# First stream: two of the three conditioning parts multiplied and added on VectorE, with one sum over partitions per 512 columns on TensorE

## The reference, cut to what matters

```python
c_act = jax.nn.silu(c)                       # c: 1 x 2048
mod = c_act @ w_ada[l] + b_ada[l]            # w_ada: 2048 x 12288
sh1, sc1, g1, sh2, sc2, g2 = jnp.split(mod[:, None, :], 6, axis=-1)
...
h = rms_norm(x, g_mix[l])                    # first block
proj = h @ w_in[l]                           # 2048 x 7536: "first stream"
q, k, v, q_idx, k_idx, w_idx = split_cols(p_dsa, DSA_SPLITS)
y_dsa = dsa_mixer(q, k, v, q_idx, k_idx, w_idx, q_gain[l], k_gain[l])
```

## Time and profile before

| | before |
|---|---|
| runs, median (lowest to highest) | 3314.17 us (3312.25 to 3314.31) |
| profiled execution | 3311.56 us |
| its span | 3309.3 us |
| mean granted clock of TensorE | 0.971 |
| first stream ends (last matmul of L302 there starts) | 445.82 us |
| TensorE busy | 3100.6 us, 94% |
| VectorE busy | 2067.7 us, 62% |
| ScalarE busy | 1508.7 us, 46% |

### The profile page before, as it was taken

How to read it: one execution, slowest core, us unless ns; L and a number is a source line. 1 busy time by engine, 2 the same in 40 slices (tenths; PEclk the granted TensorE clock), 3 DMA queues, 4 the chain that set the end, 5 groups by cost and what they waited for, 6 DMA issues and landing times. The chain is left out here.

```text
span 3309.3 us, 43832 instructions
## 1 busy us (share of the span) xinstructions
PE 3100.6 (94%) x17864; PEld 2459.1 (74%) x17864; DVE 2067.7 (62%) x2331; ACT 1508.7 (46%) x1819; POOL 20.1 (1%) x10
## 2 busy tenths in 40 slices
PE   8999957979899999999999998999998999999997
PEld 7888844947677676666688876787776788888886
DVE  4557536354677868685548857765575655555555
ACT  4335422223465656564444455455444444444443
POOL 0000001100000000000000000000000000000000
PEclk9999978989899999999999999999999999999999
DMA  7989876076787879696276653475665655555552
GB/s 270 331 274 329 274 263 249 4 296 233 259 315 267 313 256 341 229 320 212 93 248 209 208 194 126 163 241 172 240 230 191 209 185 190 186 182 190 185 183 76
DMA packets 358321, 739.09 MB, mean 223 GB/s; under 512 B 19977, under 2 KB 118422, under 8 KB 344583
## 3 DMA queue, kind: packets, MB, share of 16 engines
q1 hardware_dynamic: 342916, 711.64, 62.5%
q10 hardware_dynamic: 15236, 25.06, 2.1%
HBM read 710.00 MB, written 26.65 MB: 223 GB/s over the span
## 5 line engine op out<-in xcount | busy, mean ns | idle before, releaser
L286 DVE TENSOR_TENSOR moe_w_lo<-ring,moe_w_hi 128x1024 fp32r<-128x1024 f32 x384 | 464.0, 1222 | 174.5 <-ACT moe_w_hi L276 165.4
L286 DVE TENSOR_TENSOR mx_w_lo<-ring,mx_w_hi 128x1024 fp32r<-128x1024 f32 (+1 forms) x288 | 347.5, 1210 | 307.9 <-ACT mx_w_hi L276 303.7
L276 ACT CAST moe_w_hi<-ring 128x1024 fp32r<-128x1024 f32 x384 | 402.3, 1049 | 285.0 <-PE psum L302 281.3
L276 ACT CAST mx_w_hi<-ring 128x1024 fp32r<-128x1024 f32 (+1 forms) x288 | 297.5, 1037 | 448.0 <-PE psum L302 432.0
L286 DVE TENSOR_TENSOR mlp_w_lo<-ring,mlp_w_hi 128x1024 fp32r<-128x1024 f32 x256 | 313.5, 1225 | 293.1 <-ACT mlp_w_hi L276 292.0
L276 ACT CAST mlp_w_hi<-ring 128x1024 fp32r<-128x1024 f32 x256 | 268.4, 1049 | 418.2 <-PE psum L302 418.2
L302 PE MATMUL psum<-mx_w_hi,mx_a_hi 128*128 128x496 f32 (+1 forms) x1024 | 405.6, 396 | 6.4 <-DVE mx_w_lo L286 4.6
L302 PE MATMUL psum<-mx_w_lo,mx_a_hi 128*128 128x496 f32 (+1 forms) x1024 | 397.6, 388 | 0.0
L302 PE MATMUL psum<-mx_w_hi,mx_a_lo 128*128 128x496 f32 (+1 forms) x1024 | 397.6, 388 | 0.0
L286 DVE TENSOR_TENSOR in_w_lo<-ring,in_w_hi 128x628 fp32r<-128x628 f32 x192 | 155.3, 813 | 185.8 <-ACT in_w_hi L276 184.6
L302 PE MATMUL psum<-in_w_hi,in_a_hi 128*128 128x314 f32 x768 | 244.1, 318 | 1.4 <-DVE in_w_lo L286 1.2
(11 more groups left out here) (596 smaller groups left out, 5594.6 us busy)
## 6 DMA issues: line engine op xcount, KB each, us to landing
ring<-in_w_ada SPq DMA_DIRECT2D x72, 1024.0 KB, 7.6
ring<-in_w_e_gate SPq DMA_DIRECT2D x64, 1024.0 KB, 5.4
ring<-in_w_e_up SPq DMA_DIRECT2D x64, 1024.0 KB, 6.3
ring<-in_w_e_down SPq DMA_DIRECT2D x64, 1024.0 KB, 5.2
ring<-in_w_up SPq DMA_DIRECT2D x64, 1024.0 KB, 5.2
ring<-in_w_down SPq DMA_DIRECT2D x64, 1024.0 KB, 5.1
ring<-in_w_in SPq DMA_DIRECT2D x64, 992.0 KB, 5.1
ring<-in_w_in SPq DMA_DIRECT2D x96, 628.0 KB, 5.5
```

What stands on the lines that cost most here:

```text
L276: self.nc.scalar.copy(self.w[0][:, self._half(j, half), :, 0:cols], self.view[:, slot, ks, 0:cols]).then_inc(self.hi_done, 1)
L286: self.nc.vector.tensor_tensor(self.w[1][:, q, :, 0:cols], self.view[:, j % self.slots, ks, 0:cols], self.w[0][:, q, :, 0:cols].bitcast(F3 ...
```

## The change

For parts 0 and 2 (blocks 0 to 15 and 32 to 47) the product with c goes to VectorE. A block is now 512 rows by 512 columns, four tiles of 128 rows with 2 KB in a row, and four blocks (c = 0 to 3) with their 16 row tiles give 512 columns (b). VectorE multiplies each row tile by its column of c, per partition, and adds it to an accumulator `acc` of 128x512 (two take turns): two operations at tick(j) and two at tick(j) + 1, each waiting for the one before (`added`). After each half it waits for its own last operation. After four blocks TensorE takes the sum over partitions as one f32 matmul with 32 columns of ones, at tick(j) + 3, into 32 partitions of the same bank. So 64 matmuls of a part give way to 4. SyncE waits for `weighed` (VectorE) in place of `spent`, and for blocks after such a one at tick(j - 2) + 3 instead of + 1. ScalarE copies these parts out at tick + 3. Part 1 stays on TensorE as it was.

```diff
--- before.py
+++ after.py
@@ -542,46 +542,122 @@
         w = self.chip.dram["w_ada_2"][0]
         return w[k * P:(k + 1) * P, part * D:(part + 1) * D].rearrange("p (b n) -> p b n", n=NB)
 
-    SPARE = 48
-
-    def spares(self, st, tiles, conditioned):
-
-        self.tiles, self.conditioned = tiles, conditioned
+    SPARE, BY_VECTOR = 48, (0, 2)
+
+    def spares(self, st, tiles):
+
+        self.tiles = tiles
         self.filled, self.spent = [st.sem(f"filled{n}") for n in range(2)], st.sem("spent")
+        self.base = self.used
 
     def spare_tick(self, j):
         return 9 + 15 * j // 4
 
+    def by_vector(self, j):
+        return j // KT in self.BY_VECTOR
+
+    def sums(self, st):
+
+
+        self.acc = st.sb("acc", [P, 2, NB])
+        self.weighed, self.summed, self.added = (st.sem(f"c_{n}") for n in ("weighed", "summed", "added"))
+
     def spare_sync(self, sp):
+        turns = {True: 0, False: 0}
+        of = []
         for j in range(self.SPARE):
-            yield max(0, self.spare_tick(j - 2) + 1)
+            yield max(0, self.spare_tick(j - 2) + (3 if j >= 2 and self.by_vector(j - 2) else 1))
             if j >= 2:
-                sp.wait_ge(self.spent, j - 1)
-            sp.dma_start(self.tiles[j % 2], self.source(0, j)).then_inc(self.filled[j % 2], 16)
+                sp.wait_ge(*of[j - 2])
+            v = self.by_vector(j)
+            turns[v] += 1
+            of.append((self.weighed if v else self.spent, turns[v]))
+            if v:
+                part, q = divmod(j, KT)
+                b, c = divmod(q, KC)
+                w = self.chip.dram["w_ada_2"][0]
+                src = w[c * KC * P:(c + 1) * KC * P, part * D + b * NB:part * D + (b + 1) * NB]
+                sp.dma_start(self.tiles[j % 2], src.rearrange("(k p) n -> p k n", p=P)).then_inc(self.filled[j % 2], 16)
+            else:
+                self.spare_load(sp, j)
+
+    def spare_vector(self, ve, conditioned):
+        nc, at, n = self.chip.nc, CC["c_2"][0], 0
+        blocks = 0
+        for j in range(self.SPARE):
+            if not self.by_vector(j):
+                continue
+            b, c = divmod(j % KT, KC)
+            acc = self.acc[:, blocks % 2]
+            for half in range(2):
+                yield self.spare_tick(j) + half
+                if j == half == 0:
+                    ve.wait_ge(conditioned, 1)
+                if half == 0:
+                    ve.wait_ge(self.filled[j % 2], 16 * (j // 2 + 1))
+                    if c == 0 and blocks >= 2:
+                        ve.wait_ge(self.summed, blocks - 1)
+                for k in (2 * half, 2 * half + 1):
+                    w, m = self.tiles[j % 2][:, k], self.chip.cols[:, at + c * KC + k:at + c * KC + k + 1]
+                    if c == k == 0:
+                        ins = nc.vector.tensor_scalar(acc, w, m, None, ALU.mult)
+                    else:
+                        ve.wait_ge(self.added, n)
+                        ins = nc.vector.scalar_tensor_tensor(acc, w, m, acc, ALU.mult, ALU.add)
+                    ins.then_inc(self.added, 1)
+                    n += 1
+            ve.wait_ge(self.added, n)
+            ve.sem_inc(self.weighed, 1)
+            if c == KC - 1:
+                blocks += 1
+
+    def spare_load(self, sp, j):
+        sp.dma_start(self.tiles[j % 2], self.source(0, j)).then_inc(self.filled[j % 2], 16)
+
+    def spare_use(self, pe, j):
+        nc, (part, k) = self.chip.nc, divmod(self.base + j, KT)
+        if k == 0 and part:
+            pe.wait_ge(self.copied, part)
+        pe.wait_ge(self.filled[j % 2], 16 * (j // 2 + 1))
+        for b in range(4):
+            mm = nc.tensor.matmul(self.bank(part)[32 * b:32 * b + 32], self.c(k), self.tiles[j % 2][:, b],
+                                  start=(k == 0), stop=(k == KT - 1))
+        mm.then_inc(self.spent, 1)
 
     def spare_tensor(self, pe):
-        nc = self.chip.nc
+        blocks, n = 0, 0
         for j in range(self.SPARE):
-            part, k = divmod(j, KT)
-            yield self.spare_tick(j)
-            if j == 0:
-                pe.wait_ge(self.conditioned, 1)
-            if k == 0 and part:
+            part, q = divmod(j, KT)
+            if not self.by_vector(j):
+                yield self.spare_tick(j)
+                self.spare_use(pe, j)
+                continue
+            b, c = divmod(q, KC)
+            n += 1
+            if c < KC - 1:
+                continue
+            yield self.spare_tick(j) + 3
+            if b == 0 and part:
                 pe.wait_ge(self.copied, part)
-            pe.wait_ge(self.filled[j % 2], 16 * (j // 2 + 1))
-            for b in range(4):
-                mm = nc.tensor.matmul(self.bank(part)[32 * b:32 * b + 32], self.c(k), self.tiles[j % 2][:, b],
-                                      start=(k == 0), stop=(k == KT - 1))
-            mm.then_inc(self.spent, 1)
+            pe.wait_ge(self.weighed, n)
+            self.chip.nc.tensor.matmul(self.bank(part)[32 * b:32 * b + 32], self.chip.c("ones")[:, 0:32],
+                                       self.acc[:, blocks % 2], start=True, stop=True).then_inc(self.summed, 1)
+            blocks += 1
 
     def spare_scalar(self, sc):
+        turns = {True: 0, False: 0}
         for part in range(self.SPARE // KT):
-            yield self.spare_tick(part * KT + KT - 1) + 1
-            sc.wait_ge(self.spent, part * KT + KT)
+            v = part in self.BY_VECTOR
+            turns[v] += 1
+            yield self.spare_tick(part * KT + KT - 1) + (3 if v else 1)
+            if v:
+                sc.wait_ge(self.summed, 4 * turns[v])
+            else:
+                sc.wait_ge(self.spent, KT * turns[v])
             self.row_out(sc)
 
-    def spared(self):
-        self.used = self.loaded = self.SPARE
+    def spared(self, n):
+        self.used = self.loaded = self.base + n
 
     def begin(self):
         ring = self.chip.ring
@@ -3273,7 +3349,8 @@
 
         da = SparseAttention(chip, st, pool, flat[:, FEW * KC * NB:], qkT, actT, in_dram)
         ada.spares(st, (st.sb("spare", [P, 4, NB])[:],
-                        flat[:, FEW * KC * W1:FEW * KC * W1 + 4 * NB].rearrange("p (b n) -> p b n", n=NB)), conditioned)
+                        flat[:, FEW * KC * W1:FEW * KC * W1 + 4 * NB].rearrange("p (b n) -> p b n", n=NB)))
+        ada.sums(st)
         with nc.Block() as block:
             @block.sync
             def _(sp):
@@ -3290,7 +3367,7 @@
                 for n in range(FEW):
                     ring.loads[n] += body // FEW - 1
                     split.done(sp, body - FEW + n)
-                sp.wait_ge(ada.spent, ada.SPARE)
+                sp.wait_ge(ada.weighed, KT * len(ada.BY_VECTOR))
                 sp.wait_ge(da.ov_left, len(da.pairs))
                 ring.first(sp, next_weights)
                 sp.wait_ge(zeroed, 16)
@@ -3345,7 +3422,7 @@
 
             @block.vector
             def _(ve):
-                tick = Ticks(da.vector(ve))
+                tick = Ticks(da.vector(ve), ada.spare_vector(ve, conditioned))
                 norm.factors(ve)
                 for q in range(KC):
                     norm.scale(q)
@@ -3357,7 +3434,7 @@
                         tick()
                 tick.rest()
         ring.used(1, body, FEW)
-        ada.spared()
+        ada.spared(ada.SPARE)
 
 
 def load_order(d):
```

## The result

The changed kernel takes 3319.44 us in the median of 14 runs (3314.32 to 3324.03), the kernel before 3312.12 us in 14 runs beside it (3309.45 to 3315.79). The ratio is 1.0024 with a 95% interval of 1.0016 to 1.0032: slower by 0.24%, some 7 to 8 us. That lies inside the forecast range (3299 to 3324) but on the other side of the median of before than the forecast. The profiled execution took 3317.08 us, its span is 3315.2 us (before 3309.3).

A forecast was written before the change was run, and what follows sets the result against it. TensorE was taken to set the first stream's end, with VectorE and the DMA close behind. Five stretches and new waits summed as -5 + 3 + 0 + 4 - 8.6 + 3 = -3.6 us, 3314.2 to 3310.6; range 3299 to 3324.

The forecast's parts named there:

- Rival D: VectorE waits for the late spare tile; at 1.5 us per block +15 us, 3329 us; chance 0.13.
- New waits: Waits at SyncE's loads, TensorE's sums and VectorE's spare tile in the first stream: 3 us for all (0 to 12).
- the eight sums at 0.3: TensorE waits for VectorE 0.2 to 0.4 us at each sum, three ticks after its block; taken as 0.3.
- stretch 2: Ticks 46 to 69: VectorE's added block work delays TensorE's first transposes for the index rows; a loss of 3 us.
- A delay of some 3 us is absorbed if VectorE has room afterwards: Ticks where VectorE makes a half chunk and a pair take 2.3 us against TensorE's 1.74; three ticks' slack covers it.
- I compare totals per stretch: Each stretch of the first stream was judged by total work per engine, such as VectorE 60.8 of 76.2 us.
- The DMA comes before TensorE, a gain of 5: Ticks 9 to 46: DMA needs 71 us, TensorE 66.5, of 76.2; gain 5 us, between 3 and 9.7.
- rival B: DMA and handovers cost nothing in the first stream: -11.3 us, 3303 us; chance 0.30.
- Stretch 4: Ticks 129 to 150: TensorE's transposes of k wait for VectorE, 49.8 us of work in 45.3; loss 4 us (2 to 5).
- stretch 5: Ticks 150 to 192: TensorE has ten blocks less and three sums more, VectorE's work fits; a gain of 8.6 us.
- rival E: Attention handovers in ticks 150 to 192 cost 12.5 us instead of 3: +6 us, 3320 us; chance 0.11.
- C: VectorE's work is absorbed everywhere: -29.3 us, 3285 us, only if operations are a quarter shorter than 0.742; chance 0.04.

The follow-up runs named there:

- e1: Changed kernel with sums due 8 ticks after their block instead of 3, except the last of a part; ratio to the kernel before 1.0022.
- e8: Changed kernel with only blocks 0 to 8 and 38 to 45 on VectorE, old 8 KB shape, 1024-column operations; ratio to the kernel before 0.9976.
- e10: Changed kernel with half the rows of each VectorE block loaded and used twice; ratio to the kernel before 1.0001.
- e11: Kernel before with half loads for parts 0 and 2, each tile half used twice on TensorE; stream end -0.9 us, one run.
- e9: Changed kernel with all 32 blocks in the old 8 KB shape, 1024-column operations, one group of four sums per part; ratio to the kernel before 0.9976.
- e4: Changed kernel with multiply-adds on 128 of the 512 columns, loads and sums kept; ratio to the kernel before 0.9956.

## Why the prediction failed, step by step

**What held.** TensorE's price of a block, and nearly that of a sum (below); VectorE's prices (0.742 forecast, 0.75 measured); stretch 3 (forecast 0, measured 0.0); that TensorE's first transposes would wait for VectorE (4.1 us).

What a single sum costs is read from the distance of starts, as the prediction did for a block. A sum that nothing holds up, in e1:

```profile
104.01 0.31 PE L302 MATMUL psum<-in_w_hi,in_a_lo 128*128 128x314 f32 x1
104.25 1.04 PE L643 MATMUL psum<-in_acc,const 128*32 128x512 f32 x2
105.22 0.41 PE L302 MATMUL psum<-in_w_hi,in_a_hi 128*128 128x314 f32 x1
105.47 0.31 PE L302 MATMUL psum<-in_w_lo,in_a_hi 128*128 128x314 f32 x1
```

From 104.01 to 105.47 are 1.46 us; less two places of the stream (0.29) the sum costs 1.17 us, forecast 1.1, and eight cost 9.4 instead of 8.8. That is as much as a block's four matmuls side by side (1.19). The 0.94 us worked out for a single sum from the Trainium skill ("TensorE: Matmul & The Clock Gate", section "Why this matters for your kernels") doesn't hold here: the measurement decides, 1.17.

Rival D, the spare tile late, is not seen: before the multiply-adds VectorE idles 1.4 us for each of the two tiles in the whole stream. (In e8 TensorE does wait once for that tile, 3.05 us at tick 46.)

**By stretch.** Forecast, without the 3 us for waits, against the difference between two ticks of the table:

| stretch | forecast | measured |
|---|---|---|
| 1, ticks 9 to 46 | -5 | -2.9 |
| 2, ticks 46 to 69 | +3 | +12.2 |
| 3, ticks 69 to 129 | 0 | 0.0 |
| 4, ticks 129 to 151 | +4 | +4.3 |
| 5, ticks 151 to 192 | -8.6 | -5.1 |
| sum | -6.6 | +8.5 |

**The step that failed is "New waits": 3 us (0 to 12), and in it "the eight sums at 0.3", 2.4 us.** Five sums waited 14.6 us in all. What the stream lost beyond the other terms is 8.5 + 6.6 = 15.1 us, above the upper bound of 12, and 9.2 of it lie in stretch 2. This 15.1 is a remainder: it holds the late chunk, VectorE's running dry and the slower clock as well as the sums' waits. The working behind the 0.3 was sound for a VectorE that starts each block on time: done 5.4 us after its tick, TensorE there after 5.2. It left no room for a VectorE that doesn't, and the same text said that a first half chunk comes 1.5 to 2.9 us late and that VectorE is the bound around tick 46. Nobody may be late at a handover that has no time in hand. Of the 14.6 us, 4.7 is what the early due tick costs at the end of the stream (e1).

**"A delay of some 3 us is absorbed if VectorE has room afterwards" and "I compare totals per stretch".** Totals assume that delays even out within a stretch. They don't where an engine stops another one that feeds it: VectorE was busy 38.1 of 48.7 us in ticks 46 to 63. The 37.5 us forecast for its work there was right to a microsecond; what was missing is 10 us in which it stood, 6.4 of them behind a late chunk and 2.3 behind the stopped TensorE. The prediction did count the late chunk, but at its lateness in before: VectorE gets it 4.7 us after the start of tick 46 there and 8.3 us after it in the changed kernel. So the 9.2 us are about 3.6 for this, 2.3 for running dry and 2.0 behind the transposes, where ten products ran at 1.2 GHz; the rest is rounding in the forecast and small pauses. The mechanism of stretch 2, VectorE's work ahead of the transposes, was right; its start was mis-sized.

**The DMA.** "The DMA comes before TensorE, a gain of 5" was right for stretch 1, in size too: with late sums (e1) tick 46 stands at -5.2, 2.4 us earlier than in after. It was wrong to give it no price of its own in stretch 2, where e10 gains another 1.3 us on after. Half the loads give 8.3 us in all and 0.9 us in before. That a share of 0.91 to 0.99 cost TensorE nothing in before was taken as half an argument for rival B; e10 and e11 show that the same share has a price once TensorE is faster.

**The clock.** The prediction has no term for it. The slower products and sums behind the stops are 6.6 us. Their share of the loss was not tested by itself, and where VectorE is behind anyway part of it costs nothing.

**Stretch 4 and 5.** +4 by the total of VectorE came out as +4.3, though by another way than forecast: 4.20 us of it is one sum's wait (at 345.16), and in e1 the same ticks still lose 2.9 us, in e9, with 14 us less on VectorE over both parts, they gain 2.0. In stretch 5 the remainder is 3.5 us, of which 0.95 is one sum's wait; the rest was not traced to single handovers. It is far from rival E's 12.5.

**The rivals.** C, that VectorE's work is absorbed everywhere, asked for operations a quarter shorter. e4 has them 53% shorter and gets to -13 us of -29, so shorter operations would not have been enough for C: with them the DMA is full up to tick 54. E had the right kind of cause, handovers, in the wrong stretch. That the time came out inside the range is luck: single terms of the sum missed by more than the whole forecast change.

## What to carry to other kernels

Work that is moved from the bound engine to one with free time comes with a handover back. Compare its slack with the lead that the engines run in, beside comparing totals: put it later than the lead, or once per part, and give each operation as many columns as memory allows. Here the early handover was worth 4.7 us, the bytes 8.3 and VectorE's amount of work up to 21.8, and these overlap. Before moving work, ask where the giving engine would be stopped if every feeder (VectorE, ScalarE, DMA) went that much faster; here the DMA, at a share of 0.91 to 0.99, cost 0.9 us before the change and 8.3 after it. Move it block by block: eight blocks in the stretch with room brought 6.9 of the 9.6 us that 32 could bring.

## What the runs showed of the hardware

- Idle times of TensorE of 2.05 to 4.30 us in a busy stream were followed by 1.2 GHz five times in one execution, for up to thirteen products; one of 1.39 us was not.
- A multiply-add with a column as scalar takes 0.35 us for 128 columns, 0.75 for 512, 1.28 for 1024: 1.04 ns a column and 0.22 us for each operation.
- Between the products of the stream, one f32 matmul of 512 columns into 32 output rows costs TensorE 1.17 us, four of them side by side 1.19.
- Issuing 28 of the 48 blocks' loads from GpSimd's queue instead of SyncE's made the stream 4.3 us slower; the order of loads changed with it.
